# A two-layer hybrid decoder trunk: SyncE loads x in order of need, and the first and last steps are arranged anew

## The reference

```python
def rms_norm(x, g, eps=NORM_EPS):
    xf = x.astype(jnp.float32)
    y = xf * lax.rsqrt(jnp.mean(xf * xf, axis=-1, keepdims=True) + eps)
    return (y * g.astype(jnp.float32)).astype(x.dtype)
...
    h = rms_norm(x, norm_g)
    u = h @ w_in
...
    kv = (rms_norm(c_kv, kv_a_norm) @ w_kv_b).reshape(bsz, s, MLA_HEADS, QK_NOPE + V_HEAD)
    k_nope, v = kv[..., :QK_NOPE], kv[..., QK_NOPE:]
...
    y = jnp.concatenate([o_mla, o_conv, o_ssd], axis=-1) @ w_out
    return x + y
```

## Time and profile before

| | |
|---|---|
| median of 3 runs | 1558.3 us (1558.18 to 1559.57) |
| the profiled execution: its own time | 1560.33 us |
| its span in the profile | 1558.5 us |
| TensorE busy | 1525.9 us, 98% of the span |
| VectorE busy | 1007.0 us, 65% |
| ScalarE busy | 687.6 us, 44% |
| GpSimd busy | 44.7 us, 3% |
| read and written in HBM | 148.50 MB and 8.44 MB, mean 101 GB/s |

### The profile page before, as it was taken

The page is one execution under the profiler, slowest core; times in us unless marked ns, Lnnn a source line. Parts: engine busy times, 40 slices in busy tenths (PEclk is TensorE's granted clock), DMA queues, the critical chain, the costliest instruction groups (busy, mean ns, idle before and its releaser), DMA issues.

```text
span 1558.5 us, 18374 instructions
## 1 busy us (share of the span) xinstructions
PE 1525.9 (98%) x7062; PEld 1222.7 (78%) x7062; DVE 1007.0 (65%) x1496; ACT 687.6 (44%) x1014; POOL 44.7 (3%) x86
## 2 busy tenths in 40 slices
PE   7999999999999999999999999999999999999997
PEld 6777777778888887888887777778878887878885
DVE  7534674889998777443455456758999977762221
ACT  6445553434456645121253555533444575451110
POOL 0000000000000000110000000000000000000110
PEclk9999999999999999999999999999999999999999
DMA  6322222222233223544432222222223333234441
GB/s 224 94 92 81 82 82 81 68 82 68 81 111 114 89 83 96 176 142 142 142 102 78 87 89 82 95 68 68 77 73 102 99 116 98 88 99 158 150 140 62
DMA packets 44423, 158.13 MB, mean 101 GB/s; under 512 B 5520, under 2 KB 5808, under 8 KB 44336
## 3 DMA queue, kind: packets, MB, share of 16 engines
q1 hardware_dynamic: 36720, 129.64, 25.6%
q0 software_dynamic: 6464, 23.12, 5.1%
q10 hardware_dynamic: 1152, 4.19, 0.7%
HBM read 148.50 MB, written 8.44 MB: 101 GB/s over the span
## 4 chain that ended last, share of the span: by engine, by line
PE 84%; DVE 9%; ACT 4%; issue 1%; DMA 1%; ACTq 0%; DVEq 0%; POOL 0%; POOLq 0%
PE acc L494 19%; PE acc L496 18%; PE acc L495 18%; PE S L499 5%; PE S L494 3%; PE S L496 3%; PE S L495 3%; PE T L496 3%; PE T L494 3%; PE T L495 3%; DVE wlo L1022 2%; ACT L742 1%; PE M L499 1%; PE O L499 1%; DVE hlo L1105 1%
## 5 line engine op out<-in xcount | busy, mean ns | idle before, releaser
L494 PE MATMUL acc<-hhi,whi 128*128 128x512 f32 (+1 forms) x1504 | 600.6, 399 | 14.0 <-DVE wlo L1022 13.4
L496 PE MATMUL acc<-hhi,wlo 128*128 128x512 f32 (+1 forms) x1504 | 588.2, 391 | 0.0
L495 PE MATMUL acc<-hlo,whi 128*128 128x512 f32 (+1 forms) x1504 | 587.4, 391 | 0.0
L1022 DVE TENSOR_TENSOR wlo<-stage,whi 128x1024 fp32r<-128x1024 f32 (+2 forms) x252 | 300.7, 1196 | 411.5 <-ACT whi L754 408.1
L754 ACT ACTIVATE whi<-stage 128x1024 fp32r<-128x1024 f32 (+2 forms) x252 | 260.2, 1036 | 503.7 <-PE acc L496 281.4
L494 PEld LDWEIGHTS acc<-hhi,whi 128*128 128x128 f32 (+1 forms) x1504 | 282.2, 188 | 79.1 <-DVE wlo L1022 15.1
L496 PEld LDWEIGHTS acc<-hhi,wlo 128*128 128x128 f32 (+1 forms) x1504 | 281.8, 187 | 62.2
L495 PEld LDWEIGHTS acc<-hlo,whi 128*128 128x128 f32 (+1 forms) x1504 | 282.3, 188 | 60.8 <-issue 2.9
L1077 DVE SCALAR_TENSOR_TENSOR cacc<-glu,pv,cacc 128x512 f32<-128x512 f32 x240 | 168.8, 747 | 4.3 <-DVE cols L1161 0.3
L742 ACT ACT_TABLE_LOAD x67 | 86.0, 1283 | 7.5 <-issue 5.2
L494 PE MATMUL S<-hhi,whi 128*128 128x512 f32 x192 | 75.2, 392 | 0.0
(11 more groups left out here) (231 smaller groups left out, 1554.2 us busy)
## 6 DMA issues: line engine op xcount, KB each, us to landing
stage<-weights SPq DMA_DIRECT2D x236, 512.0 KB, 3.4
y_features<-xg POOLq DMA_DIRECT2D x32, 256.0 KB, 4.2
acsb<-acs_rows POOLq DMA_DIRECT2D x16, 384.0 KB, 4.1
xg<-x_features ACTq DMA_DIRECT2D x8, 512.0 KB, 9.3
xr<-x_features POOLq DMA_DIRECT2D x16, 256.0 KB, 4.1
xr<-y_features POOLq DMA_DIRECT2D x16, 256.0 KB, 4.1
stage<-weights SPq DMA_DIRECT2D x8, 256.0 KB, 2.6
stage<-weights SPq DMA_DIRECT2D x4, 384.0 KB, 3.0
```

What stands on the lines that cost most here:

```text
L494: nc.tensor.matmul(out, a, c, start=start, stop=False)
L495: nc.tensor.matmul(out, a, d, start=False, stop=False)
L496: return nc.tensor.matmul(out, b, c, start=False, stop=stop)
L1022: nc.vector.tensor_tensor(wlo[u % RING][:, 0:w], stage[u % STAGE][:, 0:w], whi[u % RING][:, 0:w].bitcast(F32), ALU.subtract).then_inc(lo_d ...
```

## The change

Ten parts. (1) SP loads x, in nine transfers between the weight units: tiles 0 and 1 alone, then pairs. (2) Unit 0 is loaded and split in two halves with semaphores of their own; PE starts when the first half is split, and waits for the second ahead of tile 2. (3) ACT issues no transfer. (4) PE runs twelve float32 matmuls of `ones` into bank M at the start. (5) Unit 1 is split ahead of tile 4 and unit 2 ahead of tile 8, as before, but unit 0 around tiles 0 and 1. (6) Three squares of x and their additions come behind tile 7, three behind tile 11, the other ten stay behind unit 4's split. (7) The squares have four buffers. (8) SP's transfers for tiles 10 to 15 come behind the load of unit 2. (9) PE's wait for `lat_r` at 2 ahead of "v" 0 goes, in both layers. (10) The last two output tiles are stored by SP, in layer 1 alone.

```diff
+FIRST_RUN = 12
+X_LOADS = [(0, 1), (1, 2)] + [(k, k + 2) for k in range(2, KX, 2)]
...
+        X_SQUARES = [temp[:, :], temp2[:, :], sqc, sqkv]
...
         @block.sync
         def _(sp):
+            def load_x(i):
+
+                k, end = X_LOADS[i]
+                sp.dma_start(xg[:, k:end, :], x[:, k * SEQ:end * SEQ].rearrange("p (k t) -> p k t", k=end - k)
+                             ).then_inc(x_loaded[i].sem, 16)
+
             sp.dma_start(pvn[:, :], params[0:P, :]).then_inc(params_loaded.sem, 16)
+            load_x(0)
             for layer in range(DEPTH):
                 for name, args, own in STEPS:
                     for u in own:
 
                         sp.wait_ge(lo_done.sem, lo_done.at(layer, u - STAGE + 1))
                         src = weights[layer:layer + 1, STARTS[u]:STARTS[u + 1]].rearrange("o (p w) -> (o p) w", p=P)
+                        if layer == 0 and u == 0:
+                            sp.dma_start(stage[0][:, 0:512], src[:, 0:512]).then_inc(half_loaded, 16)
+                            load_x(1)
+                            sp.dma_start(stage[0][:, 512:1024], src[:, 512:1024]).then_inc(stage_loaded[0].sem, 16)
+                            load_x(2)
+                            continue
                         sp.dma_start(stage[u % STAGE][:, 0:WIDTHS[u]], src).then_inc(stage_loaded[u % STAGE].sem, 16)
+                        if layer == 0 and u == 1:
+                            for i in range(3, 6):
+                                load_x(i)
+                        if layer == 0 and u == 2:
+                            for i in range(6, 9):
+                                load_x(i)
...
+            for f in (KX - 2, KX - 1):
+                sp.wait_ge(x_ready.sem, x_ready.at(DEPTH - 1, f + 1))
+                sp.dma_start(out[:, f * SEQ:(f + 1) * SEQ], xg[:, f, :]).then_inc(last_stored, 16)
             sp.wait_ge(params_loaded.sem, params_loaded.at(DEPTH - 1, 0))
+            sp.wait_ge(x_stored.sem, x_stored.at(DEPTH - 1, 16 * (KX - 2)))
+            sp.wait_ge(last_stored, 32)
...
+                if layer < DEPTH - 1:
+                    for f in (KX - 2, KX - 1):
...
         @block.tensor
...
             pe.sem_inc(unit_used.sem, RING)
+            pe.wait_ge(first_set, 3)
+            for _ in range(FIRST_RUN):
+                full(M[:, 0:P], ones[:, :], ones[:, :])
...
-                        pe.wait_ge(lo_done.sem, lo_done.at(layer, u + 1))
+                        if layer == 0 and u == 0:
+                            pe.wait_ge(half_lo, 1)
+                        else:
+                            pe.wait_ge(lo_done.sem, lo_done.at(layer, u + 1))
...
                             pe.wait_ge(h_lo.sem, h_lo.at(layer, k + 1))
+                            if layer == 0 and k == 2:
+                                pe.wait_ge(lo_done.sem, lo_done.at(0, 1))
...
                             pe.wait_ge(lat_lo.sem, lat_lo.at(layer, 6))
-                            pe.wait_ge(lat_r.sem, lat_r.at(layer, 2))
...
         @block.scalar
         def _(act):
-            for i in range(8):
-                act.dma_start(xg[:, 2 * i:2 * i + 2, :], x[:, 2 * i * SEQ:(2 * i + 2) * SEQ]
-                              .rearrange("p (k t) -> p k t", k=2)).then_inc(x_loaded[i].sem, 16)
...
-                    for k in range(12):
-                        if k in (1, 4, 8):
-                            split((1, 4, 8).index(k))
+                    x_hi_loaded(0)
+                    act.wait_ge(half_loaded, 16)
+                    nc.scalar.activation(whi[0][:, 0:512], stage[0][:, 0:512], ACT.Copy).then_inc(half_hi, 1)
+                    x_hi_loaded(1)
+                    act.wait_ge(stage_loaded[0].sem, 16)
+                    nc.scalar.activation(whi[0][:, 512:1024], stage[0][:, 512:1024], ACT.Copy).then_inc(hi_done.sem, 1)
+                    for k in range(2, 12):
+                        if k in (4, 8):
+                            split(k // 4)
                         x_hi_loaded(k)
+                        if k in (7, 11):
+                            for i in range(3):
+                                x_square(3 * (k // 8) + i)
...
-                        for k in range(KX):
-                            t = [temp, temp2][k % 2]
-                            if k >= 2:
-                                act.wait_ge(first_added, k - 1)
-                            nc.scalar.activation(t[:, :], xg[:, k, :], ACT.Square).then_inc(first_sq, 1)
+                        for k in range(6, KX):
+                            x_square(k)
```

More of the change, by code:

```diff
@@ L324, in hybrid_kernel @@
                                                      for n in ("first_set", "first_sq", "first_added", "pool_go"))
+        half_loaded, half_hi, half_lo, last_stored = (ctx.enter_context(nc.semaphore(n))
+                                                      for n in ("half_loaded", "half_hi", "half_lo", "last_stored"))
         stage_loaded = [sig(f"stage_loaded{i}", 16 * (NU // STAGE)) for i in range(STAGE)]
-        x_loaded = [sig(f"x_loaded{i}", 0) for i in range(8)]
+        x_loaded = [sig(f"x_loaded{i}", 0) for i in range(9)]
         const_loaded = sig("const_loaded", 0)
@@ L481, in _ @@
                             pool.dma_start(out[:, (f - 2) * SEQ:(f - 1) * SEQ], xg[:, f - 2, :]).then_inc(x_stored.sem, 16)
[L482 to L488, removed]
+                if layer < DEPTH - 1:
+                    for f in (KX - 2, KX - 1):
+                        pool.wait_ge(x_ready.sem, x_ready.at(layer, f + 1))
+                        go()
+                        pool.dma_start(out[:, f * SEQ:(f + 1) * SEQ], xg[:, f, :]).then_inc(x_stored.sem, 16)
+                    pool.wait_ge(x_stored.sem, x_stored.at(layer, 16 * KX))
+                    pool.sem_inc(x_free.sem, 1)
         @block.tensor
@@ L774, in x_hi_loaded, with x_square @@
                 def x_hi_loaded(k):
-                    if k % 2 == 0:
-                        act.wait_ge(x_loaded[k // 2].sem, 16)
+                    for i, (first, end) in enumerate(X_LOADS):
+                        if k == first:
+                            act.wait_ge(x_loaded[i].sem, 16)
                     x_hi(k)
+                def x_square(k):
+                    if k >= 4:
+                        act.wait_ge(first_added, k - 3)
+                    nc.scalar.activation(X_SQUARES[k % 4], xg[:, k, :], ACT.Square).then_inc(first_sq, 1)
                 if layer == 0:
@@ L1092, in x_lo, with x_add @@
                                                    op1=ALU.subtract).then_inc(h_lo.sem, 1)
+                def x_add(k):
+                    dve.wait_ge(first_sq, k + 1)
+                    if k == 0:
+                        nc.vector.tensor_copy(sqx, X_SQUARES[0]).then_inc(first_added, 1)
+                    else:
+                        dve.wait_ge(first_added, k)
+                        nc.vector.tensor_tensor(sqx, sqx, X_SQUARES[k % 4], ALU.add).then_inc(first_added, 1)
                 if layer == 0:
                     half_taps(0)
-                    for k in range(12):
-                        if k in (1, 4, 8):
-                            split((1, 4, 8).index(k))
+                    x_lo(0, 0)
+                    dve.wait_ge(half_hi, 1)
+                    nc.vector.tensor_tensor(wlo[0][:, 0:512], stage[0][:, 0:512], whi[0][:, 0:512].bitcast(F32),
+                                            ALU.subtract).then_inc(half_lo, 1)
+                    x_lo(1, 0)
+                    dve.wait_ge(hi_done.sem, 1)
+                    nc.vector.tensor_tensor(wlo[0][:, 512:1024], stage[0][:, 512:1024],
+                                            whi[0][:, 512:1024].bitcast(F32), ALU.subtract).then_inc(lo_done.sem, 1)
+                    for k in range(2, 12):
+                        if k in (4, 8):
+                            split(k // 4)
                         x_lo(k, 0)
+                        if k in (7, 11):
+                            for i in range(3):
+                                x_add(3 * (k // 8) + i)
                 def split_branch(first, end):
@@ L1174, in _ @@
                     if name == "first" and args == (1,) and layer == 0:
[L1175 to L1182, removed]
+                        for k in range(6, KX):
+                            x_add(k)
                         dve.wait_ge(first_added, KX)
```

## The result

The changed kernel takes 1549.49 us (median of 4 runs, 1548.83 to 1550.43) beside 1558.93 for the one before on the same chip: ratio 0.9937, 95% interval 0.9924 to 0.9949. That is 9.4 us gained where 5.5 had been forecast, and outside the range. The profiled execution took 1550.43 us with a span of 1548.6, 9.9 less than the span before, so the traces show the gain whole.

What follows compares the result with a forecast made beforehand. PE's own rate bounds the kernel, with the start set by a chain through DVE. Start 4.8, values 0.3 and tail 0.4 sum to 5.5 us, from 1558.3 to 1552.8 us; 8-in-10 range 1550.6 to 1554.9.

Steps and rivals of the forecast that it cites:

- start: From launch to "cq_sum": the DVE chain to the end of unit 5's split finishes 4.8 us earlier (4.2 to 5.3).
- values: Without PE's `lat_r` wait "v" 0 starts 1.1 us earlier, but "v" 1 waits for bank S0: 0.3 us (0 to 2.5).
- end: Last output tiles: SP issues and lands the stores sooner than POOL, worth 0.4 us (0 to 0.9).
- The rest to the span's end is of the program.: After the last store's landing: the remaining time belongs to the program, so no gain was counted there.
- The chain through DVE: Start: splits, x rests and additions on DVE, 26.65 us from unit 1's split without a hole, set "cq_sum", not PE.
- the landings of unit 1 at 8.55 and of tile 3 at 7.3: Start loads on SP's queue: unit 1 lands at 8.55 us instead of 9.7, tile 3 at 7.3.
- the moved sum: Start: data moved at 206 GB/s for 5 us, then 419; 2.22 MB up to unit 1 by 7.85 us.
- the window I used to clear the single queue: 17.6 to 19 us before the change: SP's queue, 133 of 135 packets, at 424 GB/s, so one queue carries the full rate.
- A (cold PE): Start: PE still at 1.2 GHz after the `ones`, 1.2 us lost, 1554.0 us; chance 0.16.
- B (late loads): Start: unit 2 lands at 17.2 as before, total gain 2.8 us, 1555.5 us; chance 0.12 with the nearest cases.
- C: Start: SP's single queue moves half of 419 GB/s with 2 KB rows, unit 3 lands about 33 us, 1565.1 us; chance 0.04.
- D: Values: "v" 1 doesn't wait, so they gain fully, 2.2 us more, 1550.6 us; chance 0.04.

## Why the prediction was wrong

The gain by parts, forecast and found: start 4.8 and 3.1, values 0.3 and nothing that can be told, end 0.4 and 7.3 to 7.5. In the pair of profiles compared above it is 2.4, 0.0 and 7.5, the whole 9.9.

**The step that failed is the tail:** "The rest to the span's end is of the program." The rows in front of me had the landing at 1551.4 and the span's end at 1558.5, and I took the 7.1 us between them as fixed, since no engine had an instruction in them. They belonged to the engine that had acted last. What I priced, SP's issue and landing against POOL's, was about right: 1548.16 against 1551.43 less the 2.41 of the shift is 0.9 us, the upper end of my bounds of 0 to 0.9. The Trainium skill (DMA: Bandwidth & Descriptors, Anatomy of one DMA) puts most of a transfer's fixed time at the write's receipt, in a section on the transfers that GpSimd issues; with that it fits that SP's landing, 2.0 us, is only 0.3 shorter than POOL's. On the part that I left out bears another page of the Trainium skill: Runtime: NRT & Kernel Launch, in its breakdown of preamble and postamble, lists a barrier in which all engines are waited for at the end. By that the last engine sets the end, and the runs agree; for POOL's own end they give 7.0 us. What POOL does in that time stays open.

**The start's mechanism was right, its size wrong by 1.7 us (2.4 in the first profile).** The chain through DVE bound, PE's start and the ones were worth nothing beyond it, the squares filled holes, the chain behind unit 5 was untouched (62.15 - 38.63 = 23.5 us, 23.4 before). The failing terms are the landings of unit 1 at 8.55 and of tile 3 at 7.3, which came at 11.6 and 10.4. I took the moved sum from 0 to 5 us and 419 GB/s after that from a trace with two queues and rows of 4 KB; the window I used to clear the single queue had only large rows. With 264 and 320 GB/s where 419 was assumed, DVE began at 12.8 (11.2 to 12.2 in the other profiles) and not at 9.7; the 0.56 us of wait that went with the two square buffers gave part of it back. PE's waits by the forecast, 0.8 at tile 12 and 0.8 at unit 5, came as 1.8 at tile 2, from the same cause, 0.3 at tile 12 and none at unit 5.

**The values' mechanism came as forecast:** the wait went to `value` in both layers, 2.3 us for 2.5. Of the 0.3 us nothing was left.

**One reading was incomplete.** PE was said to wait three times to speak of. The same view of before has a longer total than that for `rckv`:

```profile
PE T L655 <- ACT prob L742: 3.1, 2, 1.6
```

The change leaves these two waits alone, but a phase at the lower clock stands behind them in some executions (last section), so that PE's rate elsewhere is not the same from one execution to the next.

**The rivals.** A (cold PE) did not occur: no ones would have cost nothing either, so its price of 1.2 us was also too high. Of B (late loads) the kind happened and not the place: it had unit 2 late, for which DVE didn't wait in the changed kernel; late were tiles 2 and 3 and unit 1. C named the cause, small rows on one queue, at a size (half the rate up to unit 3, a loss) that it didn't have: 264 and 320 GB/s for 4 us, then 379 and more. D didn't happen; it would need the copy of `kr` moved. My range had no room for a larger gain because every case in it shared the one assumption on the end.

## What to carry to other kernels

Before pricing a change at a kernel's end, subtract the last landing from the span's end and ask whose time it is: here the engine whose list ends last adds 7 us if it is GpSimd and at most 0.5 if it is SyncE or ScalarE, so that the last stores and the last waits were better on SyncE. When a wait is taken away, follow the producer of the next wait on the same buffers to what stands ahead of it in its program order: if that doesn't hang on the engine set free, the time comes back there, and reordering that list is where the gain lies. A transfer rate from one mixture of queues and row sizes isn't the rate of another; at the start, where nothing hides it, that was 1 to 3 us.

## What the runs showed that I had not expected

**The end of POOL:** 7.1, 7.1, 7.0 and 7.0 us from its last act (a landing awaited, or its last transfer issued) to the end of the span, in the kernel before and three experiments.

**Small rows on one queue:** 264 to 320 GB/s for the first transfers, 395 to 420 with either larger rows or a second queue.

**A clock that falls in the middle.** After PE's wait for the first `prob` of a layer (1.98 us from matmul to transpose, in the executions with and without the fall alike) the changed kernel's next matmuls run at half pace for some 3 us, in that profile in layer 0:

```profile
235.00:237.00 2.00, 0.61 (x3) 0.18 (x1) 1.75 (x4) 0.87 (x5) 0.00 (x0) 1.00 0.00 0
237.00:239.00 2.00, 1.69 (x7) 1.28 (x8) 0.23 (x1) 1.61 (x3) 0.00 (x0) 0.89 0.64 174
239.00:241.00 2.00, 2.00 (x6) 1.53 (x5) 1.60 (x2) 0.31 (x1) 0.00 (x0) 0.50 0.28 92
241.00:243.00 2.00, 2.00 (x8) 1.62 (x7) 0.69 (x1) 0.76 (x3) 0.00 (x0) 0.76 0.77 258
```

The granted clock is 0.50, 1.2 GHz, and the whole costs 1.6 us. The time from "cq_sum" to the last addition counts these phases. In the kernels without `kr` moved it is 1481.6 to 1481.9 us in five profiles without one, 1483.2 in five with one (before and the changed kernel among them), and 1484.8 and 1484.9 in two with one in each layer (the second profile of the changed kernel among them). With `kr` moved it is 1478.9 in both profiles, without such a phase; since five other kernels have none either, they don't show that moving `kr` keeps the clock up. The Trainium skill (TensorE: Matmul & The Clock Gate, Part 1) says that idle time of PE brings the lower clock and that the point at which the clock rises varies from run to run; the rows agree on the first, and show that the fall too comes in some executions and not in others. The two phases, 3.2 us, are as large as the spread of the five runs of the changed kernel (1548.0 to 1551.5), and a gain of 1 to 2 us in one profile is no evidence by itself.
